# A mixture of experts as one list of 32-row blocks, with its result added on chip by a weighted one-hot matmul

## What is computed

```python
def run_block(args):
    e, toks = args
    xb = h[toks]
    gt, up = jnp.split(xb @ w_in[e], 2, axis=-1)      # w_in[e]: 1024 x 1024
    return (jax.nn.silu(gt) * up) @ w_out[e]          # w_out[e]: 512 x 1024
...
y = y.reshape(slots, d) * slot_gate[:, None].astype(y.dtype)
return jax.ops.segment_sum(y, slot_tok, num_segments=n)
```

## Time and profile before

| | us |
|---|---|
| median of 3 runs | 1646.93 (1640.84 to 1648.71) |
| span of the profiled execution | 1641.3, of which no other time is on record |
| TensorE busy | 1332.2 (81%) |
| VectorE, ScalarE, GpSimd busy | 338.1, 260.3, 234.5 |
| moved by DMA | 511.99 MB, mean 312 GB/s |

### The profile page before, as it was taken

How to read it: one execution, slowest core, us unless ns; L and a number is a source line. 1 busy time by engine, 2 the same in 40 slices (tenths; PEclk the granted TensorE clock), 3 DMA queues, 4 the chain that set the end, 5 groups by cost and what they waited for, 6 DMA issues and landing times.

```text
span 1641.3 us, 19111 instructions
## 1 busy us (share of the span) xinstructions
PE 1332.2 (81%) x6264; PEld 583.9 (36%) x6265; DVE 338.1 (21%) x728; ACT 260.3 (16%) x427; POOL 234.5 (14%) x365
## 2 busy tenths in 40 slices
PE   3999989968788788877785899887888888788782
PEld 1546544443222233222222676443322222222221
DVE  0192142241111111111113242332111111111113
ACT  3104210320110011011013233131101111011011
POOL 1004010021111111111111020002211111111111
PEclk8999979979999899999997799898999999999997
DMA  9322250569998699999998743738979999999994
GB/s 349 127 102 87 90 209 1 198 248 417 421 421 330 255 405 424 419 419 420 422 423 330 257 158 136 270 128 345 421 328 426 413 417 421 411 416 411 418 410 175
DMA packets 85134, 511.99 MB, mean 312 GB/s; under 512 B 15960, under 2 KB 18728, under 8 KB 60132
## 3 DMA queue, kind: packets, MB, share of 16 engines
q1 hardware_dynamic: 65696, 481.58, 72.2%
q0 software_dynamic: 13664, 22.11, 3.6%
q10 hardware_dynamic: 5732, 7.74, 1.4%
HBM read 513.68 MB, written 21.79 MB: 326 GB/s over the span
## 4 chain that ended last, share of the span: by engine, by line
DMA 52%; PE 34%; DVE 4%; ACT 4%; issue 3%; ACTq 1%; SPq 1%; POOL 0%; DVEq 0%; POOLq 0%; PEldq 0%
DMA ring<-in_expert_w_in 33%; DMA ring<-in_expert_w_out 15%; PE bank L1181 8%; PE bank L1329 5%; PE bank L1411 5%; PE bank L1247 3%; PE bank L1427 3%; DMA ring<-in_w_mod 2%; PE bank L1144 2%; PE bank L1134 2%; ACT work L864 1%; PE bank L1221 1%; ACTq L871 1%; PE bank L1310 1%; DMA actT<-h_rows,gidx_x 1%
## 5 line engine op out<-in xcount | busy, mean ns | idle before, releaser
L1411 PE MATMUL bank<-ring,work 128*64 128x512 f32 x2048 | 467.2, 601 | 98.7 <-DMA ring<-in_expert_w_in 85.4
L1411 PEld LDWEIGHTS bank<-ring,work 128*64 128x64 f32 x2048 | 141.5, 137 | 423.5 <-issue 266.5
L1427 PE MATMUL bank<-ring,work 128*64 128x512 f32 x1024 | 235.5, 602 | 67.1 <-DVE work L1745 67.1
L864 ACT ACTIVATE work<-bank 128x512 f32<-128x512 f32 (+2 forms) x164 | 80.4, 499 | 933.0 <-PE bank L1411 792.6
L1741 DVE COPY work<-bank 128x512 f32<-128x512 f32 x66 | 45.7, 692 | 567.0 <-PE bank L1400 560.3
L1427 PEld LDWEIGHTS bank<-ring,work 128*64 128x64 f32 x1024 | 68.2, 137 | 190.2 <-issue 111.0
L1181 PE MATMUL bank<-actT,ring 128*128 128x512 f32 (+1 forms) x384 | 124.3, 486 | 2.3 <-ACT actT L943 2.3
L830 POOL CAST sidx<-stab 128x1 uint32 x64 | 11.8, 184 | 647.3 <-DVE work L1749 647.3
L1749 DVE COPY work<-bank 128x512 f32<-128x512 f32 x64 | 44.3, 692 | 246.5 <-PE bank L1427 246.5
L1134 PE MATMUL bank<-ring,csil 128*32 128x512 f32 x384 | 56.9, 736 | 45.2 <-DMA ring<-in_w_mod 45.2
L1181 PEld LDWEIGHTS bank<-actT,ring 128*128 128x128 f32 x384 | 72.8, 190 | 53.0 <-issue 45.4
(11 more groups left out here) (199 smaller groups left out, 840.8 us busy)
## 6 DMA issues: line engine op xcount, KB each, us to landing
ring<-in_expert_w_in SPq DMA_DIRECT2D x128, 2048.0 KB, 10.2
ring<-in_expert_w_out SPq DMA_DIRECT2D x64, 2048.0 KB
ring<-in_w_mod SPq DMA_DIRECT2D x24, 2048.0 KB, 11.2
ring<-in_w_in SPq DMA_DIRECT2D x8, 2048.0 KB, 9.3
ring<-in_w_out SPq DMA_DIRECT2D x4, 2048.0 KB
states<-y_rows POOLq DMA_DIRECT2D x4, 1024.0 KB, 6.2
ring<-in_w_in SPq DMA_DIRECT2D x2, 1152.0 KB, 8.2
gates<-gate_rows POOLq DMA_DIRECT2D x2, 1024.0 KB
```

The costliest lines, as they stand in the source:

```text
L864: return act.activation(o, i, func, **kw)
L1411: ins = mm(bank[64 * g:64 * g + 64, :], xT[:, k, BLK * h:BLK * (h + 1)], w[:, k, 512 * g:512 * g + 512], start=h == 0 and k == 0, stop=h = ...
L1427: ins = mm(bank[64 * g:64 * g + 64, :], h_[:, k, :], w[:, k, 512 * g:512 * g + 512], start=k == 0, stop=k == 3)
```

## The change

The two paths (one block for each expert, and the extra ones) become one list of blocks of 32 rows; each expert has at least one, at most 64 in all. A row of a token is gathered as four quarters of 256 (`h_rows` in quarter rows), two blocks ahead, and copied by POOL into `xs` before TensorE transposes it. The products use four 32-column tiles of the array with 256 columns moving: 32 matmuls for the first, 16 for the second. The result `ye` stays on the chip: for each block VectorE makes `sel`, rows of the block by tokens, holding the token's weight where the row belongs to it, and TensorE multiplies `sel` with `ye` (`scatter`), four row groups with 32 rows each, one bank for each. In layer 1 the 256 tokens fit into four banks, where all blocks accumulate. In layer 0, with 512 tokens, a block scatters to two tiles, VectorE adds the four banks to `acc` in SBUF (`added`), and then the same for the other two tiles. `y_rows`, its scatters, its loads and the weights on ScalarE are gone. ScalarE copies `raw` and `ye`, and takes the silu, once for each block.

On SP, the six chunks of experts 0 and 1 no longer wait for the stored rows and the first gather; later chunks wait for the number of blocks whose first (or, for w_out, second) product is done; the next layer's w_mod waits for that alone. The small parameters of the next layer are loaded by SP in place of ScalarE. w_out's chunk is cut in runs of 4 KB in place of 16 KB. In the router, the counts come first, positions are those in the list of all blocks, `slots` is one matmul for each tile and choice instead of one for each pair of tiles and half, and a second such set, `weights`, gives the weights by row; it stands ahead of `mod_T(l, 5)`.

```diff
-BUFS = 4
-BLK = 64
-HALF = D // 2
+BLK = 32
+QTR = D // 4
+MAX_BLOCKS = 64
...
-        ewout = t_in["expert_w_out"].rearrange("l e (p k) n -> (l e) p (k n)", k=4)
+        ewout = t_in["expert_w_out"].rearrange("l e (k p) n -> (l e) p k n", k=4)
...
                 for e in range(2):
                     for c in range(3):
-                        if e == 0 and c == 2:
-                            sp.wait_ge(s_hd, 16 * (l + 1))
-                        if e == 1 and c == 0:
-                            sp.wait_ge(m_gath[0], 16 * (GATHERS[0] * l + 1))
...
+                        if s >= 2:
+                            at = chunks.where[(l, "expert", (s - 2) // 3, (s - 2) % 3)]
+                            sp.wait_ge(slot_ready[at[0]], at[1])
                         src = ewout[NE * l + e] if c == 2 else ewin[NE * l + e, c]
-                        sp.dma_start(slot[s], src).then_inc(slot_ready[s], 16)
+                        sp.dma_start(slot_view((l, "expert", e, c)) if c == 2 else slot[s], src).then_inc(slot_ready[s], 16)
+                got(sp, "D", l, "modT", 5)
+                if l + 1 < DEPTH:
+                    load_params(sp, l + 1)
...
-                        sp.wait_ge(expert_free, e0 + (NE * l + par - 1))
-                        sp.sem_inc(s_paced, 1)
+                        gone = blocks_before(sp, e0 + (par - 1))
                         for c in range(3):
+                            sp.wait_ge(b_out[l] if c == 2 else b_hid[l], gone + 0)
+                            sp.sem_inc(s_paced, 1)
                             if c == 2:
...
-                    if l and local == 2:
-                        for t in range(LAYER_T[l - 1]):
-                            sp.wait_ge(s_yin[t], 16 * yin_loads(l - 1, t))
                     if local >= 4:
...
-                        sp.wait_ge(expert_free, NE * l - (s < 3))
+                        if local == 0:
+                            most = blocks_before(sp, NE - 1)
+                            every = blocks_in_all(sp)
+                        if s == 2:
+                            sp.wait_ge(b_out[l - 1], most + 0)
+                        else:
+                            sp.wait_ge(b_hid[l - 1], (most if s < 2 else every) + 0)
+                        sp.sem_inc(s_paced, 1)
...
+                pool.wait_ge(s_tab, l + 1)
+                pool.wait_ge(s_hd, 16 * (l + 1))
+                for b in range(2):
+                    gather(b, b)
                 store_gates(5)
                 load_gates(5)
-                with pool.Fori(0, NE // BUFS) as turn:
-                    e0 = turn * BUFS
-                    for i in range(BUFS):
-                        pool.wait_ge(m_t1, e0 + (m0 + i + 1))
-                        gather((i + AHEAD) % BUFS, e0 + (i + AHEAD), e0 + ((NE + AHEAD) * l + AHEAD + i + 1))
...
-                        pool.wait_ge(m_y, e0 + (m0 + i + 2))
-                        pool.tensor_copy(sidx[:, i:i + 1], stab[:, 0, bass.ds(e0 + i, 1)]).then_inc(m_si, 1)
-                        pool.wait_ge(m_si, e0 + (NE * l + i + 1))
+                got(pool, "D", l, "blocks")
+                count = blocks_in_all(pool)
+                turns = count // 2 + 1
+                with pool.Fori(0, turns) as turn:
+                    for b in range(2):
+                        k = turn * 2 + b
+                        pool.wait_ge(b_gath[l][b], turn * 16 + 16)
+                        pool.wait_ge(b_t1[l], k + 1)
                         pool.sem_inc(s_mark, 1)
-                        pool.indirect_dma_start(
-                            out=rows_y, out_offset=bass.IndirectOffsetOnAxis(ap=sidx[:, i:i + 1], axis=0),
-                            in_=ye[:, i, :], in_offset=None,
-                            bounds_check=4 * nt * P - 1, oob_is_err=False).then_inc(m_scat[i], 16)
...
-                for t in range(nt):
-                    if t == 2:
-                        pool.wait_ge(expert_free, NE * (l + 1))
-                    src = yd[0:4 * nt * P, :].rearrange("(j t p h) n -> t p j (h n)", j=2, t=nt, h=2)[t]
-                    pool.dma_start(yin[t], src).then_inc(s_yin[t], 16)
+                        pool.tensor_copy(xs, xg[:, b, :]).then_inc(b_xs[l], 1)
+                        pool.wait_ge(b_xs[l], k + 1)
+                        pool.sem_inc(s_mark, 1)
+                        gather(b, k + 2)
...
+                got(act, "D", l, "blocks")
+                count = blocks_in_all(act)
+                with act.Fori(0, count) as k:
+                    act.wait_ge(b_hid[l], k + 1)
+                    copy(raw, PS[1][:, 0:256]).then_inc(b_raw[l], 1)
+                    act.wait_ge(b_t2[l], k + 1)
+                    gate_T = PS[2][:, 0:256].rearrange("p (i n) -> p i n", i=2)[:, :, 0:2 * BLK]
+                    copy(sil, gate_T, ACT.Silu).then_inc(b_sil[l], 1)
+                    act.wait_ge(b_out[l], k + 1)
+                    copy(ye, PS[3][:, 0:256]).then_inc(b_ye[l], 1)
...
-                def hidden(bank, xT, par, up, e0=None):
...
-                            for g in range(2):
-                                ins = mm(bank[64 * g:64 * g + 64, :], xT[:, k, BLK * h:BLK * (h + 1)],
-                                         w[:, k, 512 * g:512 * g + 512], start=h == 0 and k == 0,
+                def hidden(h, par):
+                    w = slot[3 * par + h].rearrange("p (k n) -> p k n", k=4)
...
+                        c = 4 * h + k
+                        for g in range(4):
+                            q = slice(BLK * g, BLK * (g + 1))
+                            ins = mm(PS[1][q, 0:256], xeT[:, c % 2, BLK * (c // 2):BLK * (c // 2 + 1)],
+                                     w[:, k, 256 * g:256 * (g + 1)], start=c == 0, stop=c == KT - 1)
+                    return ins
...
+                def scatter(first, start):
+                    for j in range(2):
+                        t = first + j
+                        for g in range(4):
+                            q = slice(BLK * g, BLK * (g + 1))
+                            ins = mm(PS[4 + g][:, 256 * j:256 * (j + 1)], sel[q, t * P:(t + 1) * P], ye[q, :],
+                                     start=start and j == 0, stop=True, skip_group_check=True)
+                    return ins
...
+                with pe.Fori(0, NE // 2) as turn:
+                    for par in range(2):
+                        n, first = blocks_of(pe, turn * 2 + par)
+                        with pe.Fori(0, n) as b:
+                            k = first + b
+                            pe.wait_ge(b_xeT[l], k + 1)
+                            pe.wait_ge(slot_ready[3 * par], turn * 16 + base[3 * par])
+                            hidden(0, par)
+                            pe.wait_ge(b_ye[l], k + 1)
+                            pe.wait_ge(b_sel[l], k + 1)
+                            if not whole:
+                                pe.wait_ge(b_evB[l], k + 1)
+                            scatter(0, not whole).then_inc(b_scA[l], 1)
+                            pe.wait_ge(slot_ready[3 * par + 1], turn * 16 + base[3 * par + 1])
+                            hidden(1, par).then_inc(b_hid[l], 1)
+                            pe.wait_ge(b_xs[l], k + 2)
+                            tokens_T()
+                            pe.wait_ge(b_raw[l], k + 1)
+                            hidden_T()
+                            if not whole:
+                                pe.wait_ge(b_evA[l], k + 1)
+                                scatter(2, True).then_inc(b_scB[l], 1)
+                            pe.wait_ge(b_hT[l], k + 1)
+                            pe.wait_ge(slot_ready[3 * par + 2], turn * 16 + base[3 * par + 2])
+                            back(par)
...
+            def added(l, half, fresh):
+                to = acc[:, 2 * half:2 * half + 2, :]
+                for g in range(4):
+                    v = to[:, :, 256 * g:256 * (g + 1)]
+                    part = PS[4 + g].rearrange("p (t n) -> p t n", t=2)
+                    if fresh:
+                        ins = dve.tensor_copy(v, part)
+                    else:
+                        ins = tt(v, part, v, ALU.add)
+                ins.then_inc((b_evB if half else b_evA)[l], 1)
...
+                def turn(k, fresh):
+                    if not whole:
+                        dve.wait_ge(b_scA[l], k + 1)
+                        added(l, 0, fresh)
+                    tokens(k + 1)
+                    dve.wait_ge(b_sil[l], k + 1)
+                    up = PS[2][:, 0:256].rearrange("p (i n) -> p i n", i=2)[:, :, 2 * BLK:]
+                    tt(hT, sil, up, ALU.mult).then_inc(b_hT[l], 1)
+                    dve.wait_ge((b_scA if whole else b_scB)[l], k + 1)
+                    ts(sel[:, 0:N], iota[:, 0:N], tabt[:, bass.ds(k, 1)], tabw[:, bass.ds(k, 1)], ALU.is_equal,
+                       ALU.mult).then_inc(b_sel[l], 1)
+                    if not whole:
+                        added(l, 1, fresh)
+                got(dve, "D", l, "blocks")
```

(1 more changed line is left out.)

546 lines of the change are left out of this document (226 added, 320 removed).

## The result

| | before | after |
|---|---|---|
| median of 16 runs | 1644.74 us (1640.84 to 1653.94) | 1651.01 us (1643.08 to 1658.77) |
| ratio of the two | | 1.004, 95% interval 1.0024 to 1.0056 |
| profiled execution, span | 1641.3 us | 1656.4 us |
| busy: TensorE, VectorE, ScalarE, GpSimd | 1332.2, 338.1, 260.3, 234.5 | 1302.8, 533.7, 453.4, 199.5 |
| mean granted clock of TensorE | 0.948 | 0.889 |

The forecast was 1632 us, 15 less than before; the kernel became 6.3 us slower.

A forecast was written before the change was run, and what follows sets the result against it. Expert stages were taken as bound by DMA, a pipe of 5.1 us weight chunks. Stages +2 and +13, between layers -19, end -12, cold starts +1 gave -15 us: 1632 off the 1646.93 median, range 1604 to 1672.

The forecast's parts named there:

- The price of a block: Expert stages: a 32-row block takes 9.3 us in both layers, along its longest way through TensorE and ScalarE.
- the end of layer 0's walk: Layer 0's experts, priced one by one: second product ends at 878 us, before 875.7, so +2.
- The weights' pace: Steady experts limited by weight loads: 15.37 us each in layer 0, 15.27 in layer 1.
- The starts of both stages: First expert product, behind the gates' load: 369 us instead of 356.5 in layer 0, 1128.5 instead of 1120.1 in layer 1.
- the seventh chunk: SyncE's expert weights in layer 0: this chunk needs a slot and leaves at 384 us, before at 372.12.
- the end: After the last product: copy and scatter 1.7, two tiles 5, then 7.4, making 14 us instead of 26.3: -12.
- By itself this buys nothing: Stage start: sending six chunks of experts 0 and 1 at once gains nothing, since the next chunk needs a slot.
- The results' way ... is 22 and stays below: Between the layers: adding and norming results takes 22 us, beside 25 for w_mod's products and transposes, before 44.3: -19.
- TensorE starts each stage cold and pauses more, +1: Both expert stages: cold starts and more pauses of TensorE cost 1 us in the whole sum.
- The forecast's own longest way: One block, from its first scatter through products, copy, table load of 1.28, silu and multiply: 8.9 us, plus 0.4 for the loop.
- The fourth rival: Whole kernel: no visible change, with 9.9 us a block or chunks slowed to 5.25: between -8 and +8; chance 12%.
- The second: Scatter weights load one after another, 0.107 a record; blocks 10.5 us in layer 0, 9.9 in layer 1: +17; chance 20%.

The follow-up runs named there:

- Experiment 5: Changed kernel, with VectorE adding the experts' results to the residual before it reads layer 1's first modulation columns: 1647.48 us, 1.0012 of the kernel before.
- the second profile of before: The kernel before, unedited, profiled once more in a later run: span 1645.1 us.
- the second profile: The changed kernel, unedited, timed and profiled once more: median 1649.87 us, 1.0039 of the kernel before.

## Why the prediction was wrong

**What held.** The price of a block at the full clock, 9.0 inside an expert in both layers for 9.3, and the end of layer 0's walk: last product at 876.5, forecast 878. That it came within 2 us is partly luck, since blocks at a new expert cost 0.5 to 0.9 more than 9.3 and the waits for weights were fewer than forecast. A chunk with none ahead of it landed in 7.2 us before (the one sent at 317.66), 2 more than a third of an expert's 15.48, as the walk had it. The weights' pace: SyncE's rows give (854.53 - 609.84) / 16 = 15.29 us an expert in layer 0 and (1618.99 - 1283.65) / 22 = 15.24 in layer 1, forecast 15.37 and 15.27, with the shorter runs of the second weight and without the results' way through DRAM:

```profile
382.66 1.08 SPq L714 DMA_DIRECT2D ring<-in_expert_w_in  x2
...
609.84 4.97 SPq L714 DMA_DIRECT2D ring<-in_expert_w_in  x2
...
854.53 5.58 SPq L714 DMA_DIRECT2D ring<-in_expert_w_in  x2
...
1283.65 5.89 SPq L714 DMA_DIRECT2D ring<-in_expert_w_in  x2
...
1618.99 5.42 SPq L714 DMA_DIRECT2D ring<-in_expert_w_in  x2
```

The starts of both stages (within 2 us), the seventh chunk, and the end: 14.4 for 14. "By itself this buys nothing" was about right: with the old waits the kernel is 4.6 us slower, on intervals that touch. The reason given was only half of it: the seventh chunk does wait for its slot (65 us after the first chunk, 67 with the old waits), but the slower store of the rows, 20.7 us, and the gather held up by it I had not seen.

**Step 1 that failed: "The results' way ... is 22 and stays below", -19 us between the layers.** This is the largest miss, 12 to 13 us. The durations were right (adds, adds, four tiles, norm). They were laid beside the weights' way without asking for the order on VectorE and ScalarE: a read that waits for TensorE stands ahead of the first result, and the copy for the second `mod_T` behind the norm. -6 to -7 came for -19. Experiment 5 took one of the two orders away and got 5.4 to 6.7 us back.

**Step 2 that failed: "TensorE starts each stage cold and pauses more, +1".** This term was put at next to nothing without a row behind it. The forecast's own longest way has the table load in it, so that TensorE would stand in a block of layer 1, where the second scatter is gone, follows from it; that the granted clock would be lower in a stretch with such gaps (0.89 and 0.91, and 0.98 with them filled) was not in the sum. The start of a stage is in the trace: the first half of its first product took 3.21 us, at a clock of 0.62 over the 3.6 us from 366.90 in layer 0 and of 0.61 over the 3.4 us from 1131.60 in layer 1, where later ones took 1.93, so 1.3 us each. The first fourteen blocks, forecast at 14 x 9.3 and 10 us of waits, 140.2 us, took 154.3 and 149.3 at a clock of 0.89 and 0.91; with the gap filled they took 143.4. The stage lost 11 to 16 us against before (9 to 13 against the second profile of before) where 4.7 were forecast; against the run with the gap filled, these two profiles lose 6 to 11 of it.

**Not in the forecast:** 3 to 9 us of layer 1's mixer (2 to 8 against the second profile of before). The instructions there are the same and the time goes with the clock granted; why that clock is lower in the changed kernel stays open.

Sum by the second profile, against the first of before: +11.0 at the start (49.8 - 38.8), -8.2, -6.0, +3.0, +9.1, +11.2, -11.6, and -1.4 for all ahead of it: +7.1, and the spans are 1648.2 and 1641.3. In the medians it is +6.3. The fourth rival, "nothing to be seen", was nearest in the total, but not by its mechanism; neither the pace nor a block of 9.9 in layer 0 happened. The second, which forecast layer 1 to take 9.9, is near to what layer 1 did, again for another reason: the scatter's records came 0.072 apart, not 0.107.
